# A two-block network in float32 from products of three: new tables for the order of all steps, and the attention gate of the second block's first layer projected earlier

## The reference

```python
h = jnp.einsum('bsd,de->bse', x, w_in)
(dq, dk, dv, sq, sk, sv, iq, ik, iw, fq, fk, fv, ff, gate) = split_columns(h)
a  = diff_attention(...)        # 4 heads: softmax - lam * softmax, then a norm of each head
bo = dsa_attention(...)         # 8 index heads give a score, the top 64 keys are attended
co = forgetting_attention(...)  # scores with a running sum of log gates
mixed = jnp.concatenate([a, bo, co], axis=-1) * jax.nn.silu(gate)
return layer_norm(ALPHA * x + mixed @ w_out, ln_g, ln_b)
```

```python
shift, scale, gate = split(silu(c) @ w_mod + b_mod)       # for x and for the context
hx = rms_norm(xs, norm_g) * (1 + scale) + shift
px = split_cols(hx @ w_in + b_in)
ya = (silu(layer_norm(conv31(val * sigmoid(glu)))) * silu(cgate)) @ w_conv_out   # branch 0
yb = (rms_norm(gla_scan(q, k, v, decay)) * silu(gla_g)) @ w_gla_out              # branch 1
yc = (attention(q, k, v) * silu(att_g)) @ w_attn_out                             # branch 2
xs = xs + gate * ((sigmoid(m0) * ya + sigmoid(m1) * yb + sigmoid(m2) * yc) @ w_out)
```

## Time and profile before

| | |
|---|---|
| median of 3 runs | 1288.91 us (1288.56 to 1290.16) |
| the profiled execution | 1286.08 us, span 1284.8 us |
| mean granted clock of TensorE | 0.978 |
| PE busy | 1218.5 us, 95% of the span |
| VectorE busy | 897.7 us, 70% |
| ScalarE busy | 583.1 us, 45% |
| GpSimd busy | 271.6 us, 21% |
| chain that ended last | PE 74%, DVE 14%, issue 7%, POOL 3% |
| read from HBM | 165.79 MB, 130 GB/s over the span |

### The profile page before, as it was taken

One profiled execution on the slowest core, in us unless ns is written; L12 is line 12 of the kernel. 1 busy time (PEld: TensorE's weight loads), 2 busy tenths in 40 slices (PEclk: granted clock), 3 DMA queues, 4 the chain that ended last, 5 costly groups with the idle time before them and its releaser, 6 DMA issues.

```text
span 1284.8 us, 19629 instructions
## 1 busy us (share of the span) xinstructions
PE 1218.5 (95%) x7720; PEld 999.8 (78%) x7720; DVE 897.7 (70%) x1704; ACT 583.1 (45%) x976; POOL 271.6 (21%) x215
## 2 busy tenths in 40 slices
...
PEclk9999997999998999998999999999999999999999
...
GB/s 256 199 298 187 165 276 215 157 205 148 216 125 113 147 51 49 50 83 82 67 55 77 50 67 98 98 99 90 221 176 93 97 115 83 82 83 132 149 164 115
DMA packets 49133, 168.11 MB, mean 131 GB/s; under 512 B 5841, under 2 KB 7057, under 8 KB 48785
## 3 DMA queue, kind: packets, MB, share of 16 engines
...
HBM read 165.79 MB, written 1.05 MB: 130 GB/s over the span
## 4 chain that ended last, share of the span: by engine, by line
PE 74%; DVE 14%; issue 7%; POOL 3%; ACT 1%; DMA 0%; SPq 0%; DVEq 0%; POOLq 0%; ACTq 0%
PE bank L1601 9%; PE bank L1603 8%; PE bank L1602 8%; PE bank L1583 8%; PE bank L1585 8%; PE bank L1584 8%; PE bank L1510 4%; DVE w_lo L2387 3%; PE bank L1625 3%; PE bank L1626 3%; PE bank L1627 3%; DVE conv_val L2720 2%; PE bank L1902 2%; PE bank L1928 2%; PE bank L1727 1%
## 5 line engine op out<-in xcount | busy, mean ns | idle before, releaser
L2387 DVE TENSOR_TENSOR w_lo<-w_raw,w_hi 128x1024 fp32r<-128x1024 f32 (+3 forms) x264 | 325.1, 1236 | 151.5 <-ACT w_hi L1967 149.5
L1967 ACT ACTIVATE w_hi<-w_raw 128x1024 fp32r<-128x1024 f32 (+3 forms) x264 | 269.8, 1026 | 334.6 <-issue 107.6
L1583 PE MATMUL bank<-w_hi,x_hi 128*128 128x512 f32 (+4 forms) x736 | 296.7, 403 | 12.9 <-DVE w_lo L2387 12.2
L1585 PE MATMUL bank<-w_hi,x_lo 128*128 128x512 f32 (+4 forms) x736 | 279.9, 380 | 0.0
L1584 PE MATMUL bank<-w_lo,x_hi 128*128 128x512 f32 (+4 forms) x736 | 279.6, 380 | 0.0
L1601 PE MATMUL bank<-x_hi,w_hi 128*128 128x512 f32 (+1 forms) x640 | 225.6, 352 | 0.5 <-DVE w_lo L2387 0.3
L1603 PE MATMUL bank<-x_lo,w_hi 128*128 128x512 f32 (+1 forms) x640 | 216.3, 338 | 0.0
L1602 PE MATMUL bank<-x_hi,w_lo 128*128 128x512 f32 (+1 forms) x640 | 216.2, 338 | 0.0
L1583 PEld LDWEIGHTS bank<-w_hi,x_hi 128*128 128x128 f32 x736 | 140.9, 191 | 45.1 <-DVE w_lo L2387 14.3
L1585 PEld LDWEIGHTS bank<-w_hi,x_lo 128*128 128x128 f32 x736 | 140.1, 190 | 26.8
L1584 PEld LDWEIGHTS bank<-w_lo,x_hi 128*128 128x128 f32 x736 | 140.6, 191 | 22.4
...
## 6 DMA issues: line engine op xcount, KB each, us to landing
...
```

Source lines behind the costliest of these rows:

```text
L1583: mm(out, xh[:, q, col], hi[:, kk, 0:w], start=kp == 0 and kk == 0 and not with_bias, stop=False)
L1585: ins = mm(out, xl[:, q, col], hi[:, kk, 0:w], start=False, stop=last and kk == KP - 1)
L1967: do(hi, raw, ACT.Copy).then_inc(sem["cut_hi"], 1)
L2387: v.tensor_tensor(lo, raw, hi.bitcast(F32), ALU.subtract).then_inc(sem["cut_lo"], 1)
```

## The change

There are three edits. No step is added or taken away: the same 3606 steps are issued, with the same instructions, in another order.

**The order of the chunks.** In layer 0 of block two, `AG` was projected at the head of branch 2, after branch 1. It is now projected in branch 1, between `M1A` and `project_y y1`, as it already was in layer 1. Its four weight pieces move ahead of those of `project_y y1`.

```diff
         if i == 0:
             yield from project_t(l, CGATE)
-        elif i == 2 and l < LAYERS - 1:
-            yield from project_t(l, AG)
         yield from project_t(l, first)
-        if i == BRANCHES[l][0] and l == LAYERS - 1:
+        if i == BRANCHES[l][0]:
             yield from project_t(l, AG)
```

**HASTE** goes from 35 entries to 69; some are new, some change their sign. Two lines of the old table and three of the new one:

```diff
-HASTE = {"a_t_act": -0.4, "ak_flip": 0.3, "aq_act": 1.5, "att_flip fox": 1.5, "att_s diff": 0.8, "att_t_act dsa": -0.4,
-    "att_t_act fox": 0.3, "bias1": -0.4, "conv_g": -0.4, "conv_n": -1, "conv_silu": -0.4, "conv_ve": 1.5, "ev_ag": -0.4,
...
+HASTE = {"a_t_act": -0.4, "acc_add y0": -1, "acc_add y2": -1, "ak_flip": 0.3, "aq_act": 1.5, "att_exp dsa": 0.3,
+    "att_flip fox": 1.5, "att_out dsa": -1, "att_out fox": 0.8, "att_s diff": 0.8, "att_t_act diff": 6, "att_t_act dsa": -0.4,
...
+    "ln_dve": 3, "ln_stat": 6, "load": -0.4, "loads_consts": 1.5, "lr_t": 3, "mi_add": -1, "mi_dve": 6, "mi_pow": 0.3,
```

**LENGTH** gets new numbers for some twenty kinds of step (`hr_add q` 0.96 to 3.39, `roped` 1.25 to 2.34, `ln_pow` 0.32 to 1.74, `conv_var` 3.4 to 1.89, `hr_sq` 1.25 to 0.59, `flip_hi` 0.5 to 0.36), and may now have an entry for one use of a step:

```diff
-        return LENGTH.get(step[0], 0.1)
+        return LENGTH.get(called(step), LENGTH.get(step[0], 0.1))
```

More of the change, by code:

```diff
@@ L541, in stream @@
             yield from chunks.pop(0)
-HASTE = {"a_t_act": -0.4, "ak_flip": 0.3, "aq_act": 1.5, "att_flip fox": 1.5, "att_s diff": 0.8, "att_t_act dsa": -0.4,
-    "att_t_act fox": 0.3, "bias1": -0.4, "conv_g": -0.4, "conv_n": -1, "conv_silu": -0.4, "conv_ve": 1.5, "ev_ag": -0.4,
[L546 to L549, removed]
+HASTE = {"a_t_act": -0.4, "acc_add y0": -1, "acc_add y2": -1, "ak_flip": 0.3, "aq_act": 1.5, "att_exp dsa": 0.3,
+    "att_flip fox": 1.5, "att_out dsa": -1, "att_out fox": 0.8, "att_s diff": 0.8, "att_t_act diff": 6, "att_t_act dsa": -0.4,
+    "att_t_act fox": 0.3, "att_t_dve fox": 0.8, "bias1": -0.4, "bias_sel": -1, "bias_zero": -0.4, "conv_g": -0.4, "conv_hi": 0.8,
+    "conv_lo": 3, "conv_silu": -0.4, "conv_u": -3, "conv_ve": 1.5, "ev_ag": -0.4, "ev_gate": 1.5, "ev_y y0": 0.3, "flip mix": 3,
+    "flip_hi mix": 3, "flip_hi y1": 0.3, "fox_cols": 3, "fox_e": -3, "gate_mul": 1.5, "gate_rows": 0.3, "gla_iv": 1.5,
+    "gla_ki": -0.4, "gla_ks": -0.4, "gla_kt": 0.8, "gla_m": 6, "gla_o1": 6, "gla_tot": 6, "gla_zero": -3, "heads iq": -0.4,
+    "heads_act dq": -3, "heads_dve iq": -1, "hr_add q": -3, "hr_iv k": -1, "hr_sq k": 6, "hr_sq q": -0.4, "index_iw": 1.5,
+    "ln_dve": 3, "ln_stat": 6, "load": -0.4, "loads_consts": 1.5, "lr_t": 3, "mi_add": -1, "mi_dve": 6, "mi_pow": 0.3,
+    "mi_x": -0.4, "out_add": -1, "params": -1, "project_y y0": 6, "project_y y2": 0.3, "roped": -1, "scale": 0.8, "sub_pow": -3,
+    "sub_sq": -3, "sub_sum": -0.4, "y2_gate": -1, "y2_hi": 1.5}
 def called(step):
@@ L748 @@
     "acc_add": 1.25, "ak_flip": 0.43, "ak_t": 0.6, "aq_act": 0.48, "aq_dve": 0.6, "aq_flip": 0.43, "att_exp": 1.0,
[L749 to L766, removed]
@@ L767 @@
-    "y2_gate": 1.25, "y2_hi": 0.55, "y2_lo": 0.6}
+    "att_max": 0.5, "att_max diff": 0.62, "att_norm": 0.47, "att_out": 0.34, "att_out2": 0.62, "att_out_diff": 0.87,
+    "att_t_act": 0.4, "att_t_dve": 0.35, "att_v": 0.5, "bias0": 4.5, "bias1": 4.5, "bias_sel": 1.4, "bias_zero": 1.1,
+    "conv_dev": 0.6, "conv_g": 1.25, "conv_hi": 0.33, "conv_lo": 0.79, "conv_mean": 3.4, "conv_n": 0.6, "conv_rs": 2.56,
+    "conv_sd": 0.5, "conv_silu": 0.75, "conv_sq": 0.52, "conv_u": 1.25, "conv_var": 1.89, "conv_ve": 0.6, "cut_hi": 1.0,
```

16 lines of the change are left out of this document (added).

## The result

| | before | changed |
|---|---|---|
| median | 1289.29 us (1288.56 to 1290.16, 4 runs) | 1272.68 us (1271.82 to 1272.97, 4 runs) |
| ratio, 95% interval | | 0.9868 (0.9856 to 0.9881) |
| profiled execution | 1286.08, span 1284.8 | 1272.52, span 1271.2 |
| mean granted clock of it | 0.978 | 0.983 |

A forecast was written before the change was run, and what follows sets the result against it. TensorE's 66.3 us without matmuls, mostly in a few waits, and low clock were what could be gained. Terms summed to -11.4 from 1286.1, giving 1274.7; plus 2.8 to the median, 1277.5 us, range 1268 to 1290.

The forecast's parts named there:

- Near 42 and 49 us: Block one: TensorE's waits of 1.93 us for piece 12's `w_lo` and 2.68 for the rotated heads both go, -4.6 us.
- Other `w_lo` waits: Four remaining `w_lo` waits, 4.7 us in all; near 94 us a cut now precedes index work, -1 us (0 to -2).
- Near 252 and 272 us: Waits of 2.98 and 2.58 us plus low clock shrink as cuts stand between `relu` steps, -6 us (-3 to -7).
- The rival on the weights: Earlier cuts only wait for their pieces from DMA; half of three gains is given back, 1283.3 us; chance 0.14.
- Start of block two: Near 406 us: two cuts now ahead of first-layer norm pieces on VectorE, +1 us (0 to +2.5).
- `gla_v`: Wait of 7.4 us at 596 us, for `gated` behind VectorE's convolution taps: -2 us (0 to -4), about 5.4 left.
- The end of the attention in layer 0: Block two: 5.3 us of cover between last `a_v` and branch 2's product, against a 7.0 us chain, +1.7 us.
- Layer 1: Block two: query norm wait -1 us, idle stretch from 1105 to 1131 us -3, end of the attention +1.5.
- What I can't see: Anywhere the orders differ: none to a dozen and a half small waits of 0.1 to 0.5 us, +2 (0 to +8).
- "TensorE: Matmul & The Clock Gate": Clock rival: where waits shorten, whole low stretches go, behind the 7.4 us wait and at 1105 to 1131; 1272.1 us; chance 0.10.
- The end of the attention as the bound: VectorE lacks room from 602 to 740 us, baring the 7.0 us chain in both layers; 1292.3 us, chance 0.12.
- the tables move waits only: Whole kernel: the tables move nothing that matters, waits only change places, 1289 us; chance 0.08.

## Why the prediction was right, and where its steps were off

The direction, the order of the size and the range (1268 to 1290) held: 1272.7 against 1277.5. The 4.8 us between them have two parts. The sum gave -11.4 where the profiled pair gave -13.6. And **the 2.8 us from the profiled execution to the median** were added to it; the changed kernel's profiled execution lies at its median (1272.5 and 1272.7). The step that failed there is taking that 2.8 for an offset of every kernel. The profiled execution before, at 1286.1, is under each of the 52 later runs of that kernel (1288.1 to 1290.8). Its stretch from 1018.8 to 1143.5 us is 1.9 to 4.6 us shorter than in the four other kernels with that order, so a favourable clock in layer 1 accounts for it as far as the profiles show.

By the terms, with the table above:
- *Near 42 and 49 us*, -4.6: -5.1. The kernel with piece 12's cuts ahead has -4.4 at this place, so the cause is shown. The size is that of one execution: with the same order it is -2.9 in the kernel with new tables in block one alone, where piece 12 came late.
- *Other `w_lo` waits*, -1: a lead of 1.6 more between 49.0 and 204.2 us, -1.6. Three executions with the old order differ by 2.9 us in this stretch, seven with the new one by 1.8, so the term is neither confirmed nor refuted. Only one of the four waits stands at the very start (2.9 us at 13.9), not two.
- *Between the layers*, 0: 14 us at half clock before, 10 now, about 1 us, and part of the row above.
- *Near 252 and 272 us*, -6: -4.8 by 273.3, and 0.8 given back by 335.5. Both waits for `w_lo` are gone, but one of 1.3 us for `relu` is new, and the clock is low again (0.79 from 256 to 264). The rival on the weights, that the transfers would hold the cuts back, is refuted for this place: from 240 to 246 us DMA moves 401 GB/s, and TensorE has no gap. At 42 us it came true in one execution, by the rows of the kernel with new tables in block one.
- *Start of block two*, +1: -3.6 from 335.5 to 413.6, of which -1.7 come before 398.6, still ahead of this wait, and -2.0 around it. This is the largest miss, with the wrong sign. I had priced two cuts on VectorE's queue ahead of the norm. The first step behind the norm did come 2.8 us later against the rest, but the step behind it no longer waits, and the low clock is 3.4 us shorter. I had priced neither that second wait nor the clock behind it. The kernel with the new tables in block one alone gains 2.2 us from 335.5 to 413.6, with a wait of 3.1 us for `x_lo` there, and the one with the rest alone 2.1, so each half has a part in it.
- *`gla_v`*, -2 (5.4 of 7.4 us left): -1.1 (6.7 left). The reason given, the queue of taps, was wrong. Eleven taps fewer took off 1.0 us where the same price gives 7.2. The wait is `gated` behind the query norms in VectorE's queue; moving two steps ahead of part of them took off 3.9 of the 6.7 us. With the transposes behind the moved projection, TensorE waited as long for the fourth norm itself. That `AG`'s steps don't fill it, as they stand behind the transposes, held.
- *The end of the attention in layer 0*, +1.7: +0.4, with no wait. The second `y_lo` ended at 741.45 and the product began at 741.5. The chain took 7.8 us where I had priced 7.0; the cover I gave as 5.3 us was 7.9. This term was mis-sized twice: each of the eight `gate_ones` is two rows of the trace, and they took 2.9 us in place of 1.2. And they wait for VectorE's `gate_diag` themselves, before as now, here for 0.9 us.
- *Layer 1*, -1, -3 and +1.5: in the pair of profiles +1.7 together. Against the four other kernels with the old order the changed one takes 1.0 to 3.7 us less from 1018.8 to 1143.5 us, and 0.8 more from there to branch 2's product. So together they are -0.2 to -2.9, where the terms sum to -2.5.
- *What I can't see*, +2: nothing that shows. But that unseen waits come with a new order is the finding of the study: where single steps or entries, or LENGTH alone, were changed, five of seven kernels came out 4 to 30 us slower.
- *The bounds.* I wrote that they sum to -20 and +4. By the terms as they stand it is -24.6 and +8.9; the stated range didn't rest on them.

**The rivals.** The two rules of the Trainium skill: the one in "GPSIMD Engine Reference" (Specifications) made 1 us, which no run here isolates. Of "TensorE: Matmul & The Clock Gate" (What's actually happening) I took that shorter waits would give back whole low stretches, 1272.1. It gave nearly the measured time, but by luck, not at the places I named: behind `gla_v` 7 us of low clock are left where 10 were, and around 1110 7 where 10 were; the rest went at 48, 195 and 406. I had also written that nothing comparable is lost behind waits of 2.68 us or less. But behind the one of 2.68 the clock is at 0.57 from 48 to 52 us:

```profile
48.00:52.00 4.00, 3.04 (x12) 2.81 (x13) 0.49 (x2) 2.14 (x4) 0.91 (x1) 0.57 0.64 237
```

The end of the attention as the bound did not happen, nor did the tables move waits only.
